# Decoder step, projection stage: earlier weight splits, weight loads on SyncE, value pages first on VectorE, gate chain spread out

## What is computed

```
h  = rmsnorm(x) @ w_in                       # fq fk fv ff fz | hq hf hi hz | mq mz | ga gb gm
A: fox   softmax(q k^T/8 + sum log f) v      # 8 heads x 64, log f = log_sigmoid(ff + bias)
B: hgrn  S = f*S + k v^T, o = q S            # 4 heads, state 128 x 128
M: cross attention into 256 memory tokens    # 4 heads x 128
out = x + (sig(ga)*(A*silu(fz))@w_pa + sig(gb)*(B*silu(hz))@w_pb + sig(gm)*(M*silu(mz))@w_pm) @ w_o
```

## Time and profile before

| | |
|---|---|
| median of 3 runs | 2944.14 us (2939.34 to 2949.62) |
| profiled execution | 2938.52 us, span 2936.8 us |
| the stage of the change | about 155 to 948 us of the span |
| PE busy over the span | 2781.4 us (95%) |
| DVE, ACT, POOL busy | 1579.3 us (54%), 1026.3 us (35%), 833.1 us (28%) |
| granted TensorE clock, mean | 0.984 |

### The profile page before, as it was taken

One profiled execution on the slowest core, in us unless ns is written; L12 is line 12 of the kernel. 1 busy time (PEld: TensorE's weight loads), 2 busy tenths in 40 slices (PEclk: granted clock), 3 DMA queues, 4 the chain that ended last, 5 costly groups with the idle time before them and its releaser, 6 DMA issues.

```text
span 2936.8 us, 38536 instructions
## 1 busy us (share of the span) xinstructions
PE 2781.4 (95%) x13880; PEld 2277.1 (78%) x13880; DVE 1579.3 (54%) x2995; ACT 1026.3 (35%) x1946; POOL 833.1 (28%) x835
## 2 busy tenths in 40 slices
PE   7899989999999999899899999999999998999998
PEld 5778777667777778787678877888888887888887
DVE  5414677543342567766456555556554564444444
ACT  1211111333331444443254555455444232323231
POOL 6048886234534453434020042010020134000000
PEclk9999999999999999999999999999999999999999
DMA  5666688746564666655754555555445565333431
GB/s 173 226 241 213 210 249 262 264 142 184 183 189 157 218 209 226 215 197 195 247 160 136 166 187 176 149 174 156 132 140 181 185 227 181 106 127 104 129 101 43
DMA packets 278957, 525.79 MB, mean 179 GB/s; under 512 B 110238, under 2 KB 119007, under 8 KB 256495
## 3 DMA queue, kind: packets, MB, share of 16 engines
q1 hardware_dynamic: 211407, 281.89, 30.9%
q10 hardware_dynamic: 54720, 201.19, 19.7%
q0 software_dynamic: 12640, 40.25, 4.7%
HBM read 410.82 MB, written 112.41 MB: 178 GB/s over the span
## 4 chain that ended last, share of the span: by engine, by line
PE 68%; POOL 12%; DMA 5%; issue 3%; DVE 3%; ACT 2%; SPq 1%; ACTq 0%; POOLq 0%; DVEq 0%
PE fill_out L2619 21%; POOL dc_slot L1660 4%; PE fox_o_sum L345 4%; PE fox_turned L391 4%; PE in_out L98 3%; PE in_out L100 3%; PE in_out L99 3%; PE mf_out L100 3%; PE mf_out L98 3%; PE mf_out L99 3%; PE fox_scores L379 2%; PE mf_fin L98 2%; PE mf_fin L100 2%; PE mf_fin L99 2%; PE fox_scores L380 2%
## 5 line engine op out<-in xcount | busy, mean ns | idle before, releaser
L2619 PE MATMUL fill_out<-keep_hi,fill_x 128*128 128x512 f32 x2112 | 735.3, 410 | 26.0 <-DMA fill_x<-x_tiles 14.7
L2619 PEld LDWEIGHTS fill_out<-keep_hi,fill_x 128*128 128x128 f32 x2112 | 386.1, 190 | 99.5 <-issue 20.0
L2619 PE MATMUL fill_out<-keep_lo,fill_x 128*128 128x512 f32 x1056 | 432.5, 410 | 0.0
L498 DVE TENSOR_TENSOR fox_pt_lo<-fox_turned,fox_pt_hi 128x512 fp32r<-128x512 f32 (+1 forms) x320 | 194.8, 609 | 183.9 <-ACT fox_pt_hi L443 181.5
L443 ACT ACTIVATE fox_pt_hi<-fox_turned 128x512 fp32r<-128x512 f32 (+1 forms) x320 | 169.9, 531 | 302.6 <-PE fox_turned L391 301.0
L2247 ACT ACTIVATE in_stage<-in_out 128x512 f32<-128x512 f32 (+1 forms) x119 | 71.1, 597 | 575.9 <-PE in_out L100 527.7
L2719 POOL CAST keep_hi<-fill_raw 128x512 fp32r<-128x512 f32 x72 | 48.5, 673 | 732.0 <-PE fill_out L2629 705.9
L484 DVE CUSTOM_DVE_ANT_0 fox_probs<-fox_scores,fox_bias 128x512 f32<-128x512 f32 (+2 forms) x320 | 187.5, 609 | 98.1 <-PE fox_scores L380 55.5
L2619 PEld LDWEIGHTS fill_out<-keep_lo,fill_x 128*128 128x128 f32 x1056 | 200.8, 190 | 32.3
L391 PE MATMUL fox_turned<-ident,fox_probs 128*128 128x128 f32 x1088 | 172.6, 274 | 14.9 <-ACT fox_probs L434 14.9
L391 PEld LDWEIGHTS fox_turned<-ident,fox_probs 128*128 128x128 f32 x1088 | 128.5, 140 | 45.0 <-ACT fox_probs L434 20.0
(11 more groups left out here) (396 smaller groups left out, 6494.2 us busy)
## 6 DMA issues: line engine op xcount, KB each, us to landing
fill_x<-x_tiles ACTq DMA_DIRECT2D x130, 1024.0 KB, 5.5
dc_slot<-in_cache_fox_k_dram SPq DMA_DIRECT2D x128, 256.0 KB, 3.9
dc_slot<-in_cache_fox_v_dram SPq DMA_DIRECT2D x128, 256.0 KB, 3.2
in_raw<-in_w_in_dram POOLq DMA_DIRECT2D x104, 256.0 KB, 4.0
plain<-fill_stage ACTq DMA_DIRECT2D x96, 256.0 KB, 5.1
turned<-in_stage ACTq DMA_DIRECT2D x64, 256.0 KB, 3.9
fill_raw<-in_w_in_dram SPq DMA_DIRECT2D x56, 256.0 KB, 2.8
mf_g_in<-gated SPq DMA_DIRECT2D x51, 256.0 KB, 3.4
```

The source lines that it names most:

```text
L498: dve.tensor_tensor(pt_lo[:, b, skip:BANK], bank_of(st)[:, skip:BANK], pt_hi[:, b, skip:BANK].bitcast(F32), ALU.subtract).then_inc(turned_ ...
L2619: ins = pe.matmul(self.out[n % self.OUTS][:], x, w, start=(k == 0 and term == 0), stop=(ends and term == 2))
```

## The change

Five edits:

1. `split_at` returns `max(0, k - 2)` instead of `k` for the slices that are not bound to the last unit: slices 0, 1, 2 in the first unit, then one per unit, the last two units empty. Slices 4 to 7 of the second pass's groups stay where they are.
2. The raw slices are loaded by SP instead of POOL: the first three at the head of SP's program, each later one at the end of the unit in which the slice three before it is split, behind a wait for that split.
3. DVE runs `low` first in a unit, ahead of sample rows, recurrence and the rest.
4. The suffix steps of the cached log gates come one unit later (3, 4, 5 become 4, 5, 6).
5. The steps of the gate chain are spread: ACT's logarithm unit 68 to 69; DVE's steps 67, 68, 69, 71 to 68, 70, 71, 74; PE's 70, 71, 75 to 72, 73, 78; SP's stores 73 to 76.

```diff
 # Decode
+    def lows(self, dve, t):
+        for n in self.tasks_at(t - 1, self.K, 2 * self.K):
+            self.low(dve, n)
 # Decode.vector
-        if t == 4:
+        if t == 5:
...
-        for n in self.tasks_at(t - 1, self.K, 2 * self.K):
-            self.low(dve, n)
 # Decode.tensor
-        if t == 3:
+        if t == 4:
...
-        if t == 5:
+        if t == 6:
 # ForgetGates.sync
-        if t == self.CHAIN + 7:
+        if t == self.CHAIN + 10:
 # ForgetGates.tensor
-        if t == self.CHAIN + 4:
+        if t == self.CHAIN + 6:
...
-        if t == self.CHAIN + 5:
+        if t == self.CHAIN + 7:
...
-        if t == self.CHAIN + 9:
+        if t == self.CHAIN + 12:
 # ForgetGates.scalar
-        if t == self.CHAIN + 2:
+        if t == self.CHAIN + 3:
 # ForgetGates.vector
-        if t == self.CHAIN + 1:
+        if t == self.CHAIN + 2:
...
-        if t == self.CHAIN + 2:
+        if t == self.CHAIN + 4:
...
-        if t == self.CHAIN + 3:
+        if t == self.CHAIN + 5:
...
-        if t == self.CHAIN + 5:
+        if t == self.CHAIN + 8:
 # project_and_decode, split_at
-            return (n - 1) * U + k
+            return (n - 1) * U + max(0, k - 2)
 # sync
+            for m in range(KT, KT + RAWS):
+                load_raw(m)
             for t in range(TICKS):
...
                 decode.sync(sp, t)
+                for m in range(KT, SLICES - RAWS):
+                    if split_at(m) == t:
+                        sp.wait_ge(split, m - KT + 1)
+                        load_raw(m + RAWS)
 # gpsimd, split_slice
-                if m + RAWS < SLICES:
-                    pool.wait_ge(split, m - KT + 1)
-                    load_raw(m + RAWS)
...
-            for m in range(KT, KT + RAWS):
-                load_raw(m)
 # vector
             for t in range(TICKS):
+                decode.lows(dve, t)
                 sums.vector(dve, t)
```

More of the change, by code:

```diff
@@ L2142, in _, with load_raw @@
         def _(sp):
+            def load_raw(m):
+                rows_ = slice(m % KT * P, (m % KT + 1) * P)
+                column = groups[group_at[first_use[m // KT]]].column if m < LOADS * KT else 0
+                sp.dma_start(raw[m % RAWS][:], w_in[rows_, column:column + W] if m < LOADS * KT else next_weights[rows_, :]
+                               ).then_inc(raw_loaded[m % RAWS], 16)
+            for m in range(KT, KT + RAWS):
+                load_raw(m)
             for t in range(TICKS):
@@ L2155, in _ @@
                 decode.sync(sp, t)
+                for m in range(KT, SLICES - RAWS):
+                    if split_at(m) == t:
+                        sp.wait_ge(split, m - KT + 1)
+                        load_raw(m + RAWS)
         @block.gpsimd
         def _(pool):
-            def load_raw(m):
-                rows_ = slice(m % KT * P, (m % KT + 1) * P)
-                column = groups[group_at[first_use[m // KT]]].column if m < LOADS * KT else 0
-                pool.dma_start(raw[m % RAWS][:], w_in[rows_, column:column + W] if m < LOADS * KT else next_weights[rows_, :]
-                               ).then_inc(raw_loaded[m % RAWS], 16)
             def split_slice(m):
```

## The result

| | before | changed |
|---|---|---|
| median | 2944.14 us | 2924.58 us (5 runs, 2921.01 to 2926.06) |
| ratio | | 0.9926 (0.9912 to 0.9941) |
| span of the profiled execution | 2936.8 us | 2919.3 us |
| last matmul group of the stage ends at | 947.7 us | 926.1 us |
| from there to the end | 1989.1 us | 1993.2 us |

What follows compares the result with a forecast made beforehand. PE, busy for 95% of the span, was taken as the bound, so time could go only from its waits and low clock. Terms 23.8 + 10.8 + 5.7 + 6.4 + 1.5 = 48.2 us off 2944.1 gave 2896 us, range 2887 to 2914.

Steps and rivals of the forecast that it cites:

- Term A: First pass: sooner splits and loads off POOL remove 18.4 us of PE's split waits and 5.4 of low clock, 23.8 us.
- low clock: PE's matmuls at the 1.2 GHz level after a long wait: 1.8 us extra each, charged to six waits, 10.8 us.
- Term E: Second pass: without load issues between the four late splits, six PE waits (9.0 us) and 1.8 once go, 10.8 us.
- the landing: Fourth late raw slice, from issue on SP's queue: 2.8 us taken, wanted 4.4 us later; 4.0 would still be in time.
- SP's added work: SP's 104 raw loads, each behind a wait for a split: costed at nothing.
- Term C: First value task: lo part begins 3.9 us sooner with `low` first on DVE, plus 1.8 of low clock, 5.7 us.
- Term D: Gate chain spread: the other value wait of 4.6 us goes, plus 1.8 of low clock, 6.4 us.
- term B: Suffix steps a unit later: PE's wait for the summed log gates goes, 1.5 us.
- Rival 1: Key loop on DVE and POOL becomes the bound, wait moves to unit 49 and after; half of A lost, 2908; chance 0.12.
- Rival 2: Second pass's late slices stay late through stretched subtractions or a late raw slice; E lost, 2907 us; chance 0.15.
- Rival 3: SP, held at waits for late splits, delays value pages at 12 group starts and becomes the bound; 3003 us; chance 0.03.

Runs made afterwards that it cites:

- no_split: Changed kernel with the splits back at their old times, other four edits kept; 2907.13 us, ratio 0.9872 against the kernel before.
- raw_first: Changed kernel with SP's raw loads of a unit ahead of that unit's page loads; 2915.62 us, ratio 0.9897 against the kernel before.
- sp_only: Kernel before with only the raw slices loaded by SP instead of POOL; 2922.4 us, ratio 0.9928.
- small_only: Kernel before with only `low` first on DVE and the suffix and gate steps later; 2935.61 us, ratio 0.9961.
- loads_pool: Changed kernel with POOL issuing the raw loads again; 2939.98 us, ratio 0.9977 against the kernel before.
- second profile of the changed kernel: Changed kernel run once more, unaltered, on another chip; 2924.33 us, ratio 0.9926 against the kernel before.
- share_k: Changed kernel with splits at their old times and DVE doing one of eight key multiplications instead of one of four; 2905.97 us, ratio 0.9869 against the kernel before.
- split_only: Kernel before with only the splits two units sooner, raw slices still loaded by POOL; 2953.73 us, ratio 1.0029.
- mult_first: Changed kernel with POOL's key multiplications ahead of the unit's splits; 2920.96 us (three runs, a fourth of 5588.91 left out), ratio 0.9908 against the kernel before.

## Why the prediction was right or wrong

**Term A (23.8) is the step that failed.** Its first half held: the split waits went, all 18.4 us. The failed sentence is "three splits in the first unit of a group ... puts about 4.4 us ahead of that unit's key multiplications; ... nothing on PE reads keys before unit 49", costed at nothing. PE doesn't read keys, but it reads the recurrence from unit 33 on, which DVE makes behind the key reductions in the same order, and a row that SP loads behind the key pages. I followed the data (keys to maxima) and not the engines' queues. Measured: 12.7 - 1.2 = 11.5 us of new waits and 4.6 us of low clock, so A was 18.4 + 5.4 - 16.1 = 7.7.

A second error is in the same term. "Either part alone nearly covers it and both together do" was right, and that was the reason not to want both: part 2 alone cuts the 18.4 to 8.2, so on top of it part 1 could win only what was left. It cost more than that, 17.4 us net from `no_split` to the changed kernel.

**Term E (10.8) brought 3.8.** The size of the waits was right: in `raw_first` 8.5 of the 9.0 us go. The step that failed is "it is asked for when the first of the four is split": SP stands in value pages then and asks at 657.3 instead of 653.1. A second step was wrong without harm, the landing: "I take 2.8, the row of the queue it moves to". In the changed kernel the page's part 6 has

```profile
in_raw<-in_w_in_dram SPq DMA_DIRECT2D x104, 256.0 KB, 4.1
...
fill_raw<-in_w_in_dram SPq DMA_DIRECT2D x56, 256.0 KB, 2.9
```

so the time went with the stage, in which pages are loaded too, and not with the queue: 4.0 us before on POOL's, 4.1 now on SP's. That would have fitted within the 4.4 us.

**SP's added work** was costed at nothing because "in the key phase POOL's next work after that multiplication is this very split". That holds for one split per unit (in `no_split` no cast of the first pass waits for a raw slice of `rest`). With three loads together it fails: POOL's cast waits 6.73 us in the example above.

**Term C (5.7) brought 1.9.** The value wait fell from 5.1 to 1.1 as worked out, but the wait for `dc_sums` just ahead rose from 1.1 to 2.5, one of 0.7 for `dc_spread` came, and seven matmuls at 0.42 us still follow, at 528.4. The longer wait for `dc_sums` is not the work of this part: `sp_only`, which lacks it, has 2.1 us there, `small_only`, which has it, 1.5. That it comes when PE arrives sooner is likely, not shown.

**Term D (6.4) and term B (1.5)** came as said: no wait near the reciprocal, none for the suffix, and a mean clock of 1.00 behind 580. For B the room held beside part 1 only together with part 2 (5.0 us of suffix wait in `loads_pool`).

Together: 7.7 + 3.8 + 1.9 + 6.4 + 1.5 = 21.3 us, against 781.5 - 760.4 = 21.1 of the stage. That it fits within 0.2 us is luck, since 0.2 us a matmul is rounded; but the second profile of the changed kernel gives much the same. There A is 18.4 + 5.4 - 13.9 - 5.8 = 4.1 and E 4.5, C is 1.2 and D and B 7.9 again, together 17.7 us against 781.5 - 763.5 = 18.0.

**The rivals.** Rival 1 had the right engines and the wrong place. It said the key loop limits and half of A is given back, at unit 49; two thirds were given back, from unit 33 on. Against it I had said that POOL gets 23 us back. That took 0.30 us of waiting per slice for busy time: the issues were 15.6 us, so POOL's 142 of 176 us should have been about 150. POOL did become less busy, and yet the keys trail PE by 15.8 us instead of 10.7. Most of that is order and not load: `no_split` has all of POOL's gain and a lag of 11.6. What load adds, `share_k` shows: with less key work on DVE the lag is 8.4 and the recurrence waits are gone. Rival 2 named a raw slice that lands late, and that is what kept 5.2 us. Its other half is seen too: three of the four late subtractions near 650 take 2.10 to 2.24 us instead of 1.26. In `raw_first` all four are stretched (2.25, 2.17, 2.10 and 2.16 us), and PE waits only 0.51 us there, so that half alone did not cost the term. Its 2907 and rival 1's 2908 together would have been 2896 + 12 + 10.8 = 2919; I had allowed for both only "in part". Rival 3 did not come: in the changed kernel ACT never waited for a value page.

**The rules of the Trainium skill.** Of DMA: Bandwidth & Descriptors (Issuing engines are not separate DMA queues), the trace agrees: the landing time did not change with the issuer (4.0 and 4.1 us), and what is saved on the issuing engine is small beside it, 0.87 us a load. What does not follow is that the time saved is small: part 2 alone gave 23.6 us, since those 0.87 us lay in the order of the engine that PE waits for. Of SBUF — State Buffer (Who interferes with whom), the rows agree: DVE's state product took 2.83 us at 450.31, and 0.67 us in `no_split`. It began while a multiplication of POOL ran (449.79 to 452.58) and ended 0.56 us after it. So about 2.2 of the 6.38 us that PE waits at 454.20 are this meeting.

What stays open: whether a fourth raw buffer would make three splits in a unit harmless; it wasn't tried. Since `split_only` and `mult_first` lag as much without waits for raw slices, it is doubtful.

## What to carry to other kernels

When work is moved earlier on an engine that runs in order, price what it is moved ahead of by everything queued behind on that engine and on those that wait for it, not by who reads the delayed data. Two edits that remove the same wait don't add: measure the cheaper one (here the loads) before paying for the other. Count buffers against the burst: as many splits in a row as there are raw buffers leaves nothing in flight (23.1 us of waits for raw slices with three in a unit, 5.1 with two), though that alone is not shown to be what cost the time here.

## What I had not expected of the hardware

- The low clock follows short waits as well: after one of 2.94 us at 373.12 seven matmuls ran 0.42 us apart, after one of 1.85 us at 393.81 seven, and in `share_k` seven after one of 2.53 us at 408.81. The granted clock of these stretches is 0.50. Except for one short wait I had charged it only from 3.8 us up. The length of the wait alone doesn't decide it: after waits of 2.11 us (357.5 in `no_split`), 2.18 (777.8 in the changed kernel) and 1.78 (682.9 in the kernel before) the clock stays at 1.00.
- At the head of the stage 13 or 14 matmuls ran at the low clock in some profiles (from 153.7 us in the changed kernel) and not in others, with the same code ahead of them. They cost about 2.8 of the 4 us by which the end of unit 0 differs, and no edit explains it; no kernel was profiled both with and without them.
